# Two-block network on one core: second-layer context rows prepared in the first output projection, nine context products moved into the routing stage

## The reference, cut to what matters

```python
def ec_moe(x, w_router, w_e_gate, w_e_up, w_e_down):
    aff = jax.nn.softmax((x @ w_router).astype(jnp.float32), axis=-1)
    g, idx = lax.top_k(aff.transpose(0, 2, 1), cap)          # the routing, cap = 128 of 1024 rows
    xs = jax.vmap(lambda xb, ib: xb[ib])(x, idx)
    ...

def _layer(x, xc, ...):                                      # xc = ctx_2, 256 context rows
    h = _rmsnorm(x, norm_g) * (1.0 + scale[:, None]) + shift[:, None]
    hc = _rmsnorm(xc, norm_g) * (1.0 + scale_c) + shift_c
    parts = _split_cols(h @ w_in)                            # w_in: 1024 x 2816, 22 tiles of 128 columns
    if ctx_out:                                              # only in the first of the two layers
        parts_c = _split_cols(hc @ w_in)
    ...
```

## Time and profile before

| | us |
|---|---|
| three runs, median (lowest to highest) | 3460.45 (3457.93 to 3464.17) |
| the profiled execution's own time | 3458.4 |
| its span, first to last instruction | 3456.6 |
| PE busy in the span | 3187.8 (92%) |
| DVE, ACT, POOL busy | 1874.6, 1443.6, 652.2 |
| mean granted TensorE clock, share of full speed | 0.962 |

### The profile page before, as it was taken

How to read it: one execution, slowest core, us unless ns; L and a number is a source line. 1 busy time by engine, 2 the same in 40 slices (tenths; PEclk the granted TensorE clock), 3 DMA queues, 4 the chain that set the end, 5 groups by cost and what they waited for, 6 DMA issues and landing times. The chain is left out here.

```text
span 3456.6 us, 43145 instructions
## 1 busy us (share of the span) xinstructions
PE 3187.8 (92%) x17109; PEld 2574.5 (74%) x17109; DVE 1874.6 (54%) x2573; ACT 1443.6 (42%) x2004; POOL 652.2 (19%) x449
## 2 busy tenths in 40 slices
PE   7989999999999999893999999699998998999989
PEld 3867777778777777683887887588877776887867
DVE  4357885454434354656888888534416444153643
ACT  3223222433333344542777777431127434212740
POOL 2201001011111255201545554320000003000000
PEclk7999999999999999996999999799999998999999
DMA  6427666011010243246999999421100134111022
GB/s 204 119 56 244 204 203 194 25 39 57 31 33 30 72 120 109 101 154 234 365 388 382 384 386 372 153 63 53 40 32 14 50 114 166 59 40 54 4 74 85
DMA packets 263378, 475.97 MB, mean 138 GB/s; under 512 B 24191, under 2 KB 152312, under 8 KB 263180
## 3 DMA queue, kind: packets, MB, share of 16 engines
q1 hardware_dynamic: 237000, 410.09, 34.1%
q0 software_dynamic: 15264, 57.70, 5.0%
q10 hardware_dynamic: 10916, 5.39, 0.5%
HBM read 409.53 MB, written 63.61 MB: 137 GB/s over the span
## 5 line engine op out<-in xcount | busy, mean ns | idle before, releaser
L2755 DVE TENSOR_TENSOR exp_wl<-wts_raw,exp_wh 128x2048 fp32r<-128x2048 f32 x144 | 394.4, 2774 | 104.5 <-ACT exp_wh L2715 104.5
L2715 ACT ACTIVATE exp_wh<-wts_raw 128x2048 fp32r<-128x2048 f32 x192 | 368.1, 1919 | 195.0 <-PE exp_gate L2644 63.4
L2935 PE MATMUL pr_ps<-l_h_high,pr_wh 128*128 128x512 f32 (+1 forms) x896 | 334.3, 373 | 0.0
L2936 PE MATMUL pr_ps<-l_h_low,pr_wh 128*128 128x512 f32 (+1 forms) x896 | 329.0, 367 | 0.0
L2937 PE MATMUL pr_ps<-l_h_high,pr_wl 128*128 128x512 f32 (+1 forms) x896 | 328.7, 367 | 0.0
L2614 POOL TENSOR_TENSOR exp_wl<-wts_raw,exp_wh 128x2048 fp32r<-128x2048 f32 x48 | 228.7, 4765 | 264.8 <-ACT exp_wh L2715 264.8
L886 PE MATMUL in_ps<-iw_h_high,in_wh 128*128 128x512 f32 (+1 forms) x696 | 269.6, 387 | 0.0
L887 PE MATMUL in_ps<-iw_h_low,in_wh 128*128 128x512 f32 (+1 forms) x696 | 264.9, 381 | 0.0
L888 PE MATMUL in_ps<-iw_h_high,in_wl 128*128 128x512 f32 (+1 forms) x696 | 264.3, 380 | 0.0
L3109 DVE TENSOR_TENSOR pr_wl<-two_raw,pr_wh 128x512 fp32r<-128x512 f32 x84 | 57.7, 691 | 333.7 <-ACT pr_wh L3015 332.3
L1125 DVE SCALAR_TENSOR_TENSOR g_scratch<-g_scratch,g_c 128x512 f32<-128x512 f32 x240 | 181.8, 785 | 28.9 <-DMA g_scratch<-in_w_mod 15.0
(11 more groups left out here) (533 smaller groups left out, 7340.9 us busy)
## 6 DMA issues: line engine op xcount, KB each, us to landing
wts_raw<-in_w_e_gate SPq DMA_DIRECT2D x64, 1024.0 KB, 9.5
wts_raw<-in_w_e_up SPq DMA_DIRECT2D x64, 1024.0 KB, 9.6
wts_raw<-in_w_e_down SPq DMA_DIRECT2D x64, 1024.0 KB, 7.6
g_scratch<-in_w_mod SPq DMA_DIRECT2D x80, 512.0 KB, 4.9
two_raw<-in_w_in SPq DMA_DIRECT2D x84, 256.0 KB, 2.9
g_pre<-in_w_in SPq DMA_DIRECT2D x74, 256.0 KB, 4.7
mod_w<-in_w_mod SPq DMA_DIRECT2D x4, 2048.0 KB, 11.7
wo_w<-in_w_out SPq DMA_DIRECT2D x2, 4096.0 KB, 12.8
```

What stands on the lines that cost most here:

```text
L2715: act.activation(wh[:, m % RING], raw[:, m % RAW_RING], ACT.Copy).then_inc(high, 1)
L2755: dve.tensor_tensor(wl[:, m % RING], raw[:, m % RAW_RING], wh[:, m % RING].bitcast(F32), ALU.subtract).then_inc(low, 1)
L2935: nc.tensor.matmul(out, wh[:, slot, k, :], hi, start=h == 0 and k == 0, stop=False)
L2936: nc.tensor.matmul(out, wh[:, slot, k, :], lw, start=False, stop=False)
```

## The change

In `merge`, SP loads the 256 context rows into two free slots of the weight ring, ACT takes their squares and scales them, PE transposes them (`turn_ctx`, once inside tile 7's matmuls and once after them), ACT applies gain and shift (`ctx_out`) and SP stores the result in DRAM. In `route`, SP loads it back (1 MB) with the first four of nine weight tiles (512 KB each, in pieces of 512 bytes) ahead of `g2` and the expert units; PE multiplies the nine tiles in plain float32, 8 matmuls each, before it turns the routing's results; ACT evicts each product, issues the weight loads of tiles 4 to 8 on its own queue, and stores each product in DRAM. In `project_in`, tiles 2 to 10 of `ORDER` no longer multiply the context chunk; a stored product is loaded by SP and brought into PSUM with one matmul by the identity.

```diff
+CTX_TILES = range(2, 11)
@@ merge, SP @@
                 rows_in(1)
+                sp.wait_ge(w_low, KD)
+                for n in range(CT):
+                    sp.dma_start(xc[:, n], io["ctx_2"][n * P:(n + 1) * P, :]).then_inc(cx_in[n], 16)
                 for n in range(2, LT):
...
+                sp.wait_ge(c_out, 2 * CT)
+                sp.dma_start(g.hc_dram, hc).then_inc(g.hc_stored, 16)
@@ merge, PE @@
+                        if (n, k) == (LT - 1, 0):
+                            turn_ctx(0)
...
                     pe.wait_ge(gated, 2 * min(n + 4, LT))
+                    if n >= LT - 2:
+                        pe.wait_ge(c_out, 2 * (n - LT + 3))
...
+                def turn_ctx(n):
+                    pe.wait_ge(c_scaled, n + 1)
+                    pe.wait_ge(h2t_done, 2 * (LT - 2 + n))
+                    pe.wait_ge(gated, 2 * LT)
+                    for b in range(2):
+                        for k in range(4):
+                            mm = pe.transpose(tp[:, b, k * P:(k + 1) * P], xc[:, n, (4 * b + k) * P:(4 * b + k + 1) * P], g.ident[:])
+                        mm.then_inc(c_turned, 1)
...
                     multiply(n)
+                turn_ctx(1)
                 logits_of(LT - 2)
@@ merge, ACT @@
+                def ctx_out(n, b):
+                    act.wait_ge(c_gain, 1)
+                    act.wait_ge(c_turned, 2 * n + b + 1)
+                    for k in range(4 * b, 4 * b + 4):
+                        ins = act.activation(hc[:, k, n * P:(n + 1) * P], tp[:, b, (k % 4) * P:(k % 4 + 1) * P], ACT.Identity,
+                                             scale=cgain[:, k:k + 1], bias=g.mod2[:, 1, k:k + 1])
+                    ins.then_inc(c_out, 1)
...
+                    if n == LT - 1:
+                        ctx_out(1, 0)
                     act.wait_ge(x1_done, n + 1)
...
+                    if n >= LT - 2:
+                        for b in range(n - LT + 2, 2):
+                            ctx_out(n - LT + 2, b)
...
@@ route, SP @@
+                sp.wait_ge(g.hc_stored, 16)
+                sp.dma_start(hc[:], g.hc_dram).then_inc(hc_in, 16)
+                for j in range(C_RING):
+                    ctx_weights(sp, j)
                 sp.dma_start(g.g2[:], spread(g.modrow[0, 5 * D:6 * D])).then_inc(g.g2_in, 16)
@@ route, ACT @@
+                for j in range(len(CTX_TILES)):
+                    act.wait_ge(done, j + 1)
+                    if j >= C_RING:
+                        act.wait_ge(res_out[j % C_RING], 16 * (j // C_RING))
+                    act.activation(res[:, j % C_RING], ps[:, j % C_RING, 0:N_CTX], ACT.Copy).then_inc(evicted, 1)
+                    if j + C_RING < len(CTX_TILES):
+                        ctx_weights(act, j + C_RING)
+                    act.wait_ge(evicted, j + 1)
+                    act.dma_start(g.cx_dram[j], res[:, j % C_RING]).then_inc(res_out[j % C_RING], 16)
+                for j in range(C_RING):
+                    act.wait_ge(res_out[j], 16 * len(range(j, len(CTX_TILES), C_RING)))
@@ route, PE @@
+                pe.wait_ge(hc_in, 16)
+                for j in range(len(CTX_TILES)):
+                    pe.wait_ge(wc_in[j % C_RING], 16 * (j // C_RING + 1))
+                    if j >= C_RING:
+                        pe.wait_ge(evicted, j - C_RING + 1)
+                    accumulate(nc, ps[:, j % C_RING, 0:N_CTX], [(wc[:, j % C_RING, k], hc[:, k]) for k in range(KD)]).then_inc(done, 1)
                 pe.wait_ge(found, 1)
@@ project_in, SP @@
+                    if m % 2 == 0 and m // 2 - 2 in made[1:]:
+                        ctx_in(m // 2 - 2)
@@ project_in, PE @@
-                            if (i, h, c) not in taken_ahead:
+                            if (i, h, c) not in taken_ahead and not (i in made and c == 2):
                                 mm = part(i, h, c)
                         mm.then_inc(used, 1)
+                        if i in made and h == 0:
+                            pe.wait_ge(cx_in, 16 * (i - made[0] + 1))
+                            nc.tensor.matmul(ps[:, i % 2, 2, 0:N_CTX], g.ident[:], cx[:], start=True, stop=True).then_inc(cx_used, 1)
```

More of the change, by code:

```diff
@@ L2191, in merge @@
         aff_clear = ph.sem("aff_clear")
+        xc = g.w_out[:, 0:CT]
+        hc = g.w_out[:, CT:2 * CT].rearrange("p a n -> p (a n)").rearrange("p (k n) -> p k n", k=KD)
+        cst, cgain = ph.sb("cst", [P, 3, CT]), ph.sb("cgain", [P, KD])
+        cx_in = [ph.sem(f"cx_in{n}") for n in range(CT)]
+        c_squared, c_var, c_root, c_inv, c_gain, c_scaled, c_turned, c_out = (ph.sem(n) for n in (
+            "c_squared", "c_var", "c_root", "c_inv", "c_gain", "c_scaled", "c_turned", "c_out"))
         ss, hs = g.ss, g.hs
@@ L2357, in _ @@
                     act.activation(st[:, j, 2:3], st[:, j, 1:2], ACT.Sqrt).then_inc(root_done, 1)
+                    if n == 3:
+                        act.wait_ge(c_var, 1)
+                        act.activation(cst[:, 1, :], cst[:, 1, :], ACT.Sqrt).then_inc(c_root, 1)
+                    if n >= LT - 2:
+                        for b in range(n - LT + 2, 2):
+                            ctx_out(n - LT + 2, b)
                     tile_high(n + 2)
                     scale(n + 4, range(ML_HEADS))
+                    if n == 2:
+                        for t in range(CT):
+                            act.wait_ge(cx_in[t], 16)
+                            if t:
+                                act.wait_ge(c_squared, t)
+                            act.activation(junk[:], xc[:, t], ACT.Square, accum_out=cst[:, 0, t:t + 1]).then_inc(c_squared, 1)
+                    if n == 4:
+                        act.wait_ge(c_inv, 1)
+                        for t in range(CT):
+                            act.activation(xc[:, t], xc[:, t], ACT.Copy, scale=cst[:, 2, t:t + 1]).then_inc(c_scaled, 1)
                     if n:
@@ L2456, in _ @@
                     add(n + 3)
+                    if n == 3:
+                        dve.wait_ge(c_squared, CT)
+                        dve.tensor_scalar(cst[:, 1, :], cst[:, 0, :], 1.0 / D, EPS, ALU.mult, ALU.add).then_inc(c_var, 1)
+                        dve.scalar_tensor_tensor(cgain[:], g.mod2[:, 1, KD:2 * KD], 1.0, g.pb[:, PB_NORM:PB_NORM + KD], ALU.add,
+                                                 ALU.mult).then_inc(c_gain, 1)
+                    if n == 4:
+                        dve.wait_ge(c_root, 1)
+                        dve.reciprocal(cst[:, 2, :], cst[:, 1, :]).then_inc(c_inv, 1)
                     if n == 0:
@@ L2513 @@
 HALF_ROWS = 32 + N_EXP
+C_RING = 4
 def route(nc, g):
@@ L2528, in route, with ctx_weights @@
         dve_step, found, turned = (ph.sem(n) for n in ("dve_step", "found", "turned"))
+        ph.sems.append(g.hc_stored)
+        hc = ph.sb("hc", [P, KD, N_CTX])
+        wc, res = ph.sb("wc", [P, C_RING, KD, P]), ph.sb("res", [P, C_RING, N_CTX])
+        ps = ph.ps("ps", [P, C_RING, BANK])
+        hc_in, done, evicted = (ph.sem(n) for n in ("hc_in", "done", "evicted"))
+        wc_in = [ph.sem(f"wc_in{j}") for j in range(C_RING)]
+        res_out = [ph.sem(f"res_out{j}") for j in range(C_RING)]
+        def ctx_weights(eng, j):
+            col = ORDER[CTX_TILES[j]] * P
+            eng.dma_start(wc[:, j % C_RING], g.io["w_in_2"][0].rearrange("(k p) n -> p k n", p=P)[:, :, col:col + P]
+                          ).then_inc(wc_in[j % C_RING], 16)
         with nc.Block(no_gpsimd_drain=True) as block:
@@ L2555, in _ @@
                 step(dve.tensor_copy(g.gidx[:], diff[:]))
+            @block.scalar
+            def _(act):
+                for j in range(len(CTX_TILES)):
[9 more added lines that the diff above has]
+                    act.wait_ge(res_out[j], 16 * len(range(j, len(CTX_TILES), C_RING)))
             @block.tensor
             def _(pe):
+                pe.wait_ge(hc_in, 16)
[4 more added lines that the diff above has]
+                    accumulate(nc, ps[:, j % C_RING, 0:N_CTX], [(wc[:, j % C_RING, k], hc[:, k]) for k in range(KD)]).then_inc(done, 1)
                 pe.wait_ge(found, 1)
@@ L2860, in project_in @@
         zp = g.parts[:, ZF_AT:ZF_AT + 2, :]
+        made = () if last else CTX_TILES
+        cx, cx_in, cx_used = None if last else ph.sb("cx", [P, N_CTX]), ph.sem("cx_in"), ph.sem("cx_used")
         freed = [ph.sem(f"freed{j}") for j in range(2)]
@@ L2896, in first_tiles, with ctx_in @@
                     sp.dma_start(sin[:], io["t_sin"]).then_inc(cs_in, 16)
+                def ctx_in(i):
+                    if i > made[0]:
+                        sp.wait_ge(cx_used, i - made[0])
+                    sp.dma_start(cx[:], g.cx_dram[i - made[0]]).then_inc(cx_in, 16)
                 norm.sync(sp, first_tiles)
+                if not last:
+                    ctx_in(made[0])
                 for m in range(HALF_RING, 2 * len(ORDER)):
+                    if m % 2 == 0 and m // 2 - 2 in made[1:]:
+                        ctx_in(m // 2 - 2)
                     if m == 2 * HALF_RING:
```

(3 more changed lines are left out.)

## The result

| | before | changed |
|---|---|---|
| median of 20 runs each, us (lowest to highest) | 3459.12 (3454.07 to 3464.17) | 3464.41 (3459.85 to 3471.05) |
| the profiled execution's own time, us | 3458.4 | 3465.9 |
| its span, us | 3456.6 | 3464.1 |
| PE busy, us | 3187.8 | 3210.1 |
| mean granted TensorE clock | 0.962 | 0.961 |

The changed kernel is slower: the ratio is 1.0016, with a 95% interval from 1.0009 to 1.0022, which is 5.3 us (3.1 to 7.6). The forecast was 1.2 us faster, 3459 us (set against the median of three runs, 3460.45); the time lies inside the range given, but on the other side of no change.

What follows compares the result with a forecast made beforehand. PE was taken to bound the projection and DVE the routing, where late weight loads would now starve PE. -21.8 + 20.6 = -1.2 us took 3458.4 to 3457.2; with 2.05 us for the median, 3459 us, range 3444 to 3470.

Steps and rivals of the forecast that it cites:

- The projection: First layer's projection: tiles 2 to 10 lose 25.7 us of context chunks, gain 3.9 us of identity products; net -21.8 us.
- The output projection: In merge: 16 new transposes, evictions and PE's new waits before the last two row transposes; taken as +1.0 us.
- The sum's other stages: Stages outside projection, output projection and routing: the sum gave them no term.
- PE's start in the routing: PE's first tile in the routing starts at 1576.7 + 2.1 + 2.6 + 1.8 + 0.3 = 1583.5 us.
- Tiles 0 to 3: Routing, first four tiles on PE: 3.5 us each plus 2.2 us lost at half clock, ending 1589.2 to 1599.6 us.
- The landing of ACT's loads: Routing: weight tiles on ACT's queue alternate packets with SP's, 10.4 us each; tile 4's land at 1602.6, tile 5's at 1614.4 us.
- The row: Earlier trace's DMA row, 2220 to 2231 us: the two queues passed 1019 and 1101 packets, read as a 0.160 us turn.
- What ends the block: Routing's end: ACT evicts tile 8 (0.6 us), its last store lands after 4.0 us; next block starts at 1635.7 us.
- The sum: Whole program: -21.8 + 20.6 = -1.2 us, the routing's 20.6 including 1.0 from its late start.
- Sharing by bytes: Rival, routing: ACT's queue gets as many bytes as SP's, PE never runs dry; -14.7 us, 3446 us; chance 0.25.
- The longer turn: Rival, routing: a turn takes 0.24 us, +31.7 us there, +9.9 in sum, 3470 us; chance 0.19.

Runs made afterwards that it cites:

- units_late: The changed kernel, but SP issues g2 and the ten expert units only when the last of the nine weight tiles has landed: 3452.9 us, ratio to before 0.9982.
- sp_nine: The changed kernel with all nine weight tiles loaded on SP's queue ahead of g2 and the expert units, none on ACT: 3450.8 us, ratio to before 0.9976.
- sp_nine_late: sp_nine with two result slots outliving the routing, SP waiting for the last stores at the experts' end: 3451.1 us, ratio to before 0.9974.
- proj_alone: The kernel before with only the projection's part of the change, an input slice as stored product: 3437.4 us against 3458.5, ratio 0.9934.

## Why the prediction was wrong, step by step

- **The projection** (-21.8): right. -21.1 alone, 20.3 us in the trace, a tile of 11.34 us, no waits. (48 x 0.23 + 0.4 is 11.4, not 11.3; nothing hangs on it.)
- **The output projection** (+1.0): right, 1.1. **The sum's other stages** (nothing): the experts' 1.8 us are PE's clock after waits, and 1.2 of them vary without the change.
- **PE's start in the routing**: right as a sum, by luck in its terms. 1585.51 less the 1.6 us from upstream is 1583.9 (forecast 1583.5), and from SP's issue to PE's start it is 7.0 us against 6.8. But by the packets' times in the trace the first packet leaves 0.95 us after the issue, not 2.1; the context rows take 3.7 us, not 2.6; and PE starts 1.1 us after tile 0's last packet, not 0.3, an estimate that no run bears out. The 2.1 us were misread from the earlier trace rows: there the first packet left 1.3 us after the issue, and the low mean of the window came in part from the pieces behind it, which moved at 200 to 310 GB/s until 1579. **Tiles 0 to 3**: about right, 17.0 us for four against 16.1.
- **The landing of ACT's loads: this step failed.** The prediction put it as "A turn lasts 11 us / (1101 / 16) = 0.160 us, so a weight tile with its semaphore packet takes 65 x 0.160 = 10.4 us", from 2.1 us after the issue. The mechanism, one packet of each queue by turns, was right; its sizes were not. Tile 5 started at 1622.09, 1620.5 without the upstream part, instead of 1614.4: 6.1 us late. By the packets' times this is made up as follows. Tile 0's eviction, and with it the issue at 1592.22, was 0.8 us late. Tile 4's first packet left 3.6 us after its issue, behind packets of SP (in `units_late`, with nothing ahead, 1.1 us), against 2.1 taken: 1.5 us. Tile 4's packets took 12.4 us from the first to the last, against 10.4: 2.0 us. Product 0's store and tile 5's packets took 12.7 us more, against 11.8: 0.9 us. And PE started 1.2 us after the last packet, against 0.3: 0.9 us. The longer turn, 0.178 us instead of 0.160, accounts for 2.5 us of the 6.1 (139 x 0.018); the rest is what stands around the turns. All behind tile 5 moved along: tile 8 ended 5.8 us late.
- **The row could have told part of it.** The prediction divided the window by the packets of the queue that had more of them, as if every one had met a partner. A turn in which both have a packet is 11 us / (1019 / 16) = 0.173 us by the same row, the figure that the prediction itself used for SP's queue. The durations in the earlier trace rows, 0.150 us (87.1% of 16 x 11 us over 1019 packets) and 0.028, add up to 0.178; that this is the measured turn to the digit is in part chance, since in the changed kernel the durations add up to 0.185 (88.4 + 15.7 = 104.1%, so they overlap) and the turn is 0.178.
- **What ends the block**: wrong, and it took 2.1 us off the error. The last store landed in 1.7 us instead of 4.0, with the expert units through, and the end came by PE's small products and DVE's seven steps, 3.1 us behind tile 8 instead of 5.2. In `sp_nine` and `units_late`, with units in flight, the last store does end it.
- **The sum**: routing 23.2 instead of 19.6 without `merge`'s part, experts 1.8, projection 1.5 less in this pair: +5.9 instead of -1.2. So half of the miss in this pair is the routing; 1.2 of the experts' 1.8 us are chance.
- **The rivals.** Sharing by bytes is excluded by 719 to 719 packets. The Trainium skill, "DMA: Bandwidth & Descriptors", section "Queues, rings and completion order", has each DMA engine take its queues by turns, a packet of typically 9 to 17 descriptors at a time. The turns agree; but what passes at a time here is one piece of 4 KB against one of 512 bytes, and with 2 KB pieces one of those (594 to 593). The longer turn had the right direction: it was priced at 0.24 us a turn, +9.9 us in sum, and 0.178 with slower starts brought +5.3.

## What to carry to other kernels

When two queues feed the same DMA engines, price a turn as one packet of each, from a stretch in which both queues have packets all the time; small pieces beside large ones get a small share (here 0.37 of 3.12 MB). Price the time from issue to first packet and from last packet to the waiting engine as well: here they were off by as much as the turn. A wait filled with work is free only if that work's loads fit too: here the idle engine had the room, and loading the 4.7 MB of weights in a stage with idle DMA engines (0.30 busy between 1500 and 1560 us before), and keeping the rows on the chip, turned +5.3 into -18.6 us. When a stage's end is freed by delaying other transfers, ask which small transfer (a last store, a gather) then meets them.

## What was not expected of the hardware

- A transfer's issue can hold its engine: with two loads of 1024 small packets and a store queued, ACT's issues of 128 KB stores took 11.26 and 10.83 us, and its evictions stood behind them (11.35 and 11.77 us); with the same loads alone (`units_late`) such issues took 0.33 to 1.11 us.
- The same 128 KB store lands in 1.7 us with the DMA engines nearly idle (0.11 busy) and in 5.7 us among 4 KB packets; the first two gathers of 128 rows land in 4.4 and 5.3 us behind the units (changed kernel), and the first three in 7.6 to 8.8 us among them (`units_late`, `sp_nine_late`).
- PE's time at half clock (granted clock 0.50) after a wait is not fixed: at the same place of the program, the experts' first products, it was 1.0 us before, 3.6 us in the changed kernel and in `proj_alone`, and 1.0 to 4.0 us over the nine profiled executions. From 1.0 to 3.6 us costs 1.2 us, more than the output projection's whole edit.
